# Experts in teams of four with 32 places each, instead of teams of two with 64

## The chip, the cores and the metric

The kernel runs on one core of a Trainium2 chip. The metric is the device time in microseconds. A core has TensorE (PE, the matmuls; PEld is its weight load), VectorE (DVE), ScalarE (ACT), GpSimd (POOL) and SyncE (SP, which here issues every DMA), with a scratch memory of 128 partitions (SBUF) and eight accumulation banks of 128 x 512 f32 (PSUM, `ps` in the code). The engines run their own instruction streams and wait for each other with semaphores.

## The reference, cut to what matters

Two transformer blocks over 256 tokens of 1024 channels. The change touches the mixture of experts of the second block: each token picks one of four groups, and in it two of eight experts, so 512 pairs of token and expert fall on 32 experts.

```python
def hierarchical_moe(h, rg_w, rg_b, re_w, re_b, w_gate, w_up, w_down):
    xt = h.reshape(S, D)                                  # 256 x 1024
    g_logits = xt @ rg_w + rg_b                           # 4 groups
    g_top = argmax(g_logits);  g_w = softmax(g_logits)[g_top]
    e_in = (xt @ re_w + re_b).reshape(S, 4, 8)[g_top]
    e_val, e_loc = top_k(e_in, 2)
    e_w = softmax(e_val) * g_w
    e_idx = g_top * 8 + e_loc
    for every expert e, for its tokens t:                 # 32 experts
        hb = silu(xt[t] @ w_gate[e]) * (xt[t] @ w_up[e])  # 1024 -> 256
        y[t] += (hb @ w_down[e]) * weight                 # 256 -> 1024
h = h + y
h = h + sigmoid(rms_norm(h) @ ple_gate_w) * (p @ ple_proj_w)
return rms_norm(h)
```

Each expert has 3 MB of f32 weights, 96 MB in all; every one is read, whatever the routing.

## The kernel before, in words

Before the experts stand the first block and the mixers of the second. Their matmuls are split by hand: weights and data are each taken as a high and a low part (fp32r), and three products are summed (`mm3`, L1268). That part is the same in both kernels.

**Routing.** PE computes the router's logits; DVE (`routing`, L1850) makes one-hot tables, counts each token's rank in its expert, and from it a place. `FEW` (64) places belong to each expert and `TEAM` (2) experts to a team, so that a team has 128 places, one for each row of the PE array's output. The largest count of each team goes to `route_i`; each engine reads it (`busiest`, L349) and, if it is over `FEW`, runs a loop for the rest (`extra`, L1680, L1103, L2271). `psel` is the matrix that picks the tokens of two teams (256 places), made by DVE (`select`); `places` and `weighed` (`placed`, L2304, with `weigh`, L1940) take the results back to the tokens.

**Loading.** SP loads each team's weights in `CHUNKS` (3) chunks of 2048 KB: two for gate and up (`w_eg`), one for down (`w_ed`), each 8 KB to a partition and expert. `wring` has six slots, the chunks of two teams. A slot is loaded again when PE has raised `chunk_used` for it (L510). The first six chunks are loaded while the block before still runs. After the experts' chunks SP issues two loads of `w_ple`.

**The loop over 16 teams** (L1725 on PE, L1127 on ACT, L2318 on DVE). PE in order: `gate_up` for two chunks, 16 matmuls of 512 columns in f32, one for each expert and 128 channels, with the tokens as the stationary operand. Expert j writes rows 64 j to 64 j + 63 of bank 4, so each matmul uses 64 columns of the array. Then `gather(b + 2)` picks half of the channels for a pair of teams, 16 matmuls of 256 columns into banks 5 and 6. Then it transposes `he`, which ACT (silu, L1130) and DVE (the product, L2321) have made. Then comes `combine` of the team before (16 matmuls into banks 0 to 3, where the sum over all experts stands), and last `down`, 8 matmuls of 512 columns into banks 6 and 7. ACT copies banks 6 and 7 to `yh` and DVE makes the low part `yl`. A plain f32 matmul stands in the trace as two records, an fp32r one as one.

**After the loop**: the last `combine`; ACT loads its table (L1138) and splits `w_ple` (high part, L710), DVE makes the low part (L720), adds the experts' sum to `hs` (L2339), and the last matmuls and two norms follow.

Of the kernel before, what the change touches and what calls it, by code (L numbers as in the profile page):

```python
# [41 lines left out]
FEW = 64  # L42
# [5 lines left out]
CHUNKS = 3  # L48
GU_CHUNKS = 2
# [70 lines left out]
for _name, _n in CONST:  # L120
# [17 lines left out]
        "dve": ["firsts", "select", "seconds", "comb", "moved", "xb", "he", "y"]}  # L138


def bass_two_blocks(nc, a, out):
# [4 lines left out]
    with ctx:  # L146
# [11 lines left out]
        with ExitStack() as turn:  # L158
            wring = sb("wring", [P, 2 * CHUNKS, CHUNK], F32, turn)
# [54 lines left out]
        with ExitStack() as turn:  # L214
# [3 lines left out]
            psel = [sb(f"psel{i}", [P, NB, 2 * P], F32R, turn) for i in range(2)]  # L218
            pselx = sb("pselx", [P, NB, P], F32R, turn)
            moe_room = 2 * D + 2 * SEQ + 4 * NB * P + NB * P  # L220
# [67 lines left out]
        zero = take(SEQ)  # L288
        mixed = mix[:, :, :].rearrange("p a b -> p (a b)")
# [117 lines left out]
        class Over:  # L407


            def __init__(self, eng, turn, b):  # L410
                self.eng, self.turn, self.before = eng, turn, b * (ROUNDS - 1)
# [5 lines left out]
            def step(self, what):  # L417

                def after(ins):
                    ins.then_inc(sem("over_dve"), 1)  # L420
                    self.wait("dve", what)
                return after

# [4 lines left out]
        def _(sp_):  # L428
# [77 lines left out]
            def experts(b, c):  # L506

                slot = b % 2 * CHUNKS + c
                if b >= 2:
                    sp_.wait_ge(sem("chunk_used"), (b - 2) * CHUNKS + c + 1)  # L510
                team = slice(b * TEAM, (b + 1) * TEAM)
                src = a["w_eg"][team, :, c * 2048:(c + 1) * 2048] if c < GU_CHUNKS else a["w_ed"][team, :, :]
                sp_.dma_start(wring[:, slot, :].rearrange("p (e n) -> p e n", e=TEAM), src.rearrange("e p n -> p e n"))\
                   .then_inc(sem(f"chunk{slot}"), 16)
# [3 lines left out]
            for slot, i in ((0, 1), (1, 2), (2, 2), (3, 3)):  # L518
                done, count = tile_done("w_out", i)
                sp_.wait_ge(sem(done), count)  # L520
                experts(slot // CHUNKS, slot % CHUNKS)
            sp_.wait_ge(sem("wout_psum"), KD)
            for slot in (4, 5):
                experts(1, slot - CHUNKS)
            for b in range(2, TEAMS):
                for c in range(CHUNKS):
                    experts(b, c)
            for i, count in ((0, (TEAMS - 2) * CHUNKS + 1), (1, (TEAMS - 1) * CHUNKS)):
# [10 lines left out]
        def pool_groups(eng, chain, groups, done):  # L539

            for g in groups:
                eng.wait_ge(sem("h_ready"), 2 * g + 2)
                eng.wait_ge(sem("hp_padded"), 1)
# [50 lines left out]
        def conv(eng, chain, j, done):  # L594

            eng.wait_ge(sem("z_evac"), z_done("conv", j))
            eng.wait_ge(sem("zpre_padded"), 2)
# [10 lines left out]
        def _(pool):  # L608
            chain = Chain(pool, "pool_chain")
            pool.memset(ones[:, :], 1.0).then_inc(sem("ones_ready"), 1)  # L610
            pool.memset(nones[:, :], -1.0).then_inc(sem("ones_ready"), 1)
            pool.memset(hp[:, :, 0:PADT], 0.0).then_inc(sem("hp_padded"), 1)
            pool.memset(brow[0:NH, :], NEG).then_inc(sem("brow_ready"), 1)
            whole = mix[:, 0:2, :].rearrange("p a b -> p (a b)").bitcast(I32)
            pool.iota(whole[:, 0:2 * P], pattern=[[ROUNDS * P, 2], [1, P]], base=0, channel_multiplier=0)
# [6 lines left out]
            pool.tensor_copy(iota[:, :], whole[:, 0:2 * P]).then_inc(sem("iota_ready"), 1)  # L622
            pool.tensor_copy(ranks[:, :], whole[:, 2 * P:2 * P + NE + ROUNDS]).then_inc(sem("iota_ready"), 1)
# [5 lines left out]
                .then_inc(sem("sgw_masked"), 1)  # L629
# [19 lines left out]
            for s in range(2):  # L649
                pool.memset(zpre[s][0:ML_D, :, 0:3], 0.0).then_inc(sem("zpre_padded"), 1)  # L650
# [195 lines left out]
        def _(act):  # L846
# [12 lines left out]
            act.wait_ge(sem("iota_ready"), 2)  # L859
# [237 lines left out]
            def gathered(n):  # L1097
                act.wait_ge(sem("gathered"), 2 * n + 1)
                first = n % 2 * 4
                act.activation(xb[n // 2 % 2][:, first:first + 2, :].rearrange("p a n -> p (a n)"), ps[:, 5, :], ACT.Copy)\  # L1100
                   .then_inc(sem("xb_ready"), 1)

            def extra(b):  # L1103
                count = busiest(act, b)
                with act.If(count > FEW):
                    with act.Fori(0, ROUNDS - 1) as r:
# [10 lines left out]
                with act.Else():  # L1117
                    act.sem_inc(sem("over_act"), len(OVER["act"]) * (ROUNDS - 1))
# [1390 lines left out]
```

## Time and profile before

| | us |
|---|---|
| median of 3 timed runs | 1072.61 (1070.78 to 1072.77) |
| the profiled execution | 1068.52 |
| its span, first to last instruction | 1066.8 |
| PE busy in it | 974.7 (91%) |
| DVE, ACT, POOL busy | 540.2, 416.1, 155.6 |
| mean DMA rate, and in the experts' stage | 199 GB/s, 417 to 420 |
| first gate and up matmul, last down's end | 771.3, 1011.0 |

All positions in microseconds are from the start of the span. The page shows the span in 40 equal slices of 26.7 us; a digit is the busy share in tenths, and PEclk the share of TensorE's full clock that was granted. Busy time of PE is not PE at its peak. In the chain of waits, followed back from the last instruction, "issue" is time in which the engine waited for nothing that the profile shows.

### The profile page before, as it was taken

How to read it: one execution, taken by the hardware profiler on the slowest of the kernel's cores; microseconds unless marked ns; L12 is line 12 of the kernel's file. 1: busy time of each engine (PE TensorE's matmuls, PEld its weight loads, DVE VectorE, ACT ScalarE, POOL GpSimd, SP SyncE). 2: the span in 40 equal slices, each digit the busy share in tenths (PEclk: the TensorE clock that was granted, in tenths of full speed). 3: DMA queues.
4: the chain of work that ended last, by engine and by line, in shares of the span. 5: the costliest groups of instructions: out<-in, count | busy, mean ns of one | idle time of the engine just before them, and what ended most of it. 6: DMA issues, size and time to landing. Idle time of an engine off the chain costs nothing.

```text
span 1066.8 us, 16807 instructions
## 1 busy us (share of the span) xinstructions
PE 974.7 (91%) x6776; PEld 819.1 (77%) x6777; DVE 540.2 (51%) x986; ACT 416.1 (39%) x697; POOL 155.6 (15%) x216
## 2 busy tenths in 40 slices
PE   3799999998989999999969999879699999999876
PEld 2599999998869899999959999578454555545365
DVE  5655454438783655554463548574523333433254
ACT  4543333347575534434454556633211111111153
POOL 5432323011001433331120000000100000000000
PEclk8899999999989999999998999788899999999988
DMA  7435453568522254534543412049079999999601
GB/s 290 157 106 202 167 172 134 189 185 205 141 80 89 93 213 158 188 131 163 214 164 127 159 52 82 1 168 396 3 283 417 420 420 420 419 420 419 260 1 40
DMA packets 36797, 211.99 MB, mean 199 GB/s; under 512 B 2528, under 2 KB 16112, under 8 KB 17520
## 3 DMA queue, kind: packets, MB, share of 16 engines
q1 hardware_dynamic: 36720, 210.91, 52.4%
q8 instruction: 55, 0.90, 0.3%
q14 instruction: 22, 0.18, 0.1%
HBM read 209.83 MB, written 1.07 MB: 198 GB/s over the span
## 4 chain that ended last, share of the span: by engine, by line
PE 85%; DVE 7%; ACT 3%; issue 2%; POOL 2%; DMA 0%; POOLq 0%; DVEq 0%; ACTq 0%
PE ps L1268 49%; PE ps L1651 11%; PE ps L1665 5%; PE ps L1259 3%; PE ps L1674 3%; PE ps L1623 2%; PE ps L1199 2%; DVE wl L720 2%; PE ps L1624 1%; DVE mix L1779 1%; PE ps L1306 1%; PE ps L1372 1%; PE ps L1207 1%; PE ps L1609 1%; PE ps L1592 1%
## 5 line engine op out<-in xcount | busy, mean ns | idle before, releaser
L720 DVE TENSOR_TENSOR wl<-ring,wh 128x2048 fp32r<-128x2048 f32 (+3 forms) x106 | 210.3, 1987 | 193.9 <-ACT wh L710 193.9
L710 ACT ACTIVATE wh<-ring 128x2048 fp32r<-128x2048 f32 (+3 forms) x106 | 176.1, 1665 | 267.2 <-PE ps L1268 265.2
L1268 PE MATMUL ps<-xh,wh 128*128 128x256 f32 (+3 forms) x632 | 180.5, 286 | 6.4 <-DVE xl L2343 6.4
L1268 PE MATMUL ps<-xh,wl 128*128 128x256 f32 (+3 forms) x632 | 179.0, 283 | 0.0
L1268 PE MATMUL ps<-xl,wh 128*128 128x256 f32 (+3 forms) x632 | 178.8, 283 | 0.0
L1268 PEld LDWEIGHTS ps<-xh,wh 128*128 128x128 f32 (+3 forms) x632 | 117.6, 186 | 7.8 <-issue 7.5
L1268 PEld LDWEIGHTS ps<-xh,wl 128*128 128x128 f32 (+3 forms) x632 | 117.6, 186 | 0.1
L1268 PEld LDWEIGHTS ps<-xl,wh 128*128 128x128 f32 (+3 forms) x632 | 117.5, 186 | 0.0
L1268 PE MATMUL ps<-acth,wh 128*128 128x272 f32 (+1 forms) x352 | 101.1, 287 | 0.0
L1268 PE MATMUL ps<-actl,wh 128*128 128x272 f32 (+1 forms) x352 | 100.0, 284 | 0.0
L1268 PE MATMUL ps<-acth,wl 128*128 128x272 f32 (+1 forms) x352 | 100.0, 284 | 0.0
L1268 PE MATMUL ps<-xhT,wl 128*128 128x272 f32 x320 | 92.6, 289 | 0.0
L1268 PE MATMUL ps<-xlT,wh 128*128 128x272 f32 x320 | 92.2, 288 | 0.0
L1268 PE MATMUL ps<-xhT,wh 128*128 128x272 f32 x320 | 91.3, 285 | 0.0
L575 POOL TENSOR_TENSOR sq<-sq 128x256 f32<-128x256 f32 (+1 forms) x15 | 19.1, 1274 | 436.0 <-ACT sq L685 436.0
L2327 DVE TENSOR_TENSOR yl<-ps,yh 128x512 fp32r<-128x512 f32 x32 | 20.6, 686 | 91.3 <-ACT yh L1137 91.3
L1268 PEld LDWEIGHTS ps<-acth,wh 128*128 128x128 f32 x352 | 66.5, 189 | 0.2
L1268 PEld LDWEIGHTS ps<-acth,wl 128*128 128x128 f32 x352 | 66.1, 188 | 0.2
L1268 PEld LDWEIGHTS ps<-actl,wh 128*128 128x128 f32 x352 | 66.2, 188 | 0.0
L1651 PE MATMUL ps<-wring,xb_even 128*64 128x512 f32 x256 | 60.0, 607 | 4.1 <-issue 4.0
L1268 PEld LDWEIGHTS ps<-xhT,wh 128*128 128x128 f32 x320 | 60.4, 189 | 0.0
L1268 PEld LDWEIGHTS ps<-xlT,wh 128*128 128x128 f32 x320 | 60.1, 188 | 0.0
(402 smaller groups left out, 1859.5 us busy)
## 6 DMA issues: line engine op xcount, KB each, us to landing
wring<-in_w_eg SPq DMA_DIRECT2D x32, 2048.0 KB, 14.3
ring<-in_w_gu SPq DMA_DIRECT2D x22, 2048.0 KB, 8.2
wring<-in_w_ed SPq DMA_DIRECT2D x16, 2048.0 KB, 12.9
ring<-in_w_dn SPq DMA_DIRECT2D x16, 1408.0 KB, 6.1
ring<-in_w_z SPq DMA_DIRECT2D x7, 2048.0 KB, 7.7
ring<-in_w_out SPq DMA_DIRECT2D x4, 1152.0 KB, 5.2
ring<-in_w_q SPq DMA_DIRECT2D x8, 512.0 KB, 6.2
ring<-in_w_o SPq DMA_DIRECT2D x8, 512.0 KB, 16.0
```

Of the source, the lines that this page charges most:

```text
L575: pool.tensor_tensor(even, even, odd, ALU.add).then_inc(sem("sq_paired"), 1)
L710: ins = act.activation(to, src, ACT.Copy)
L720: ins = dve.tensor_tensor(to, src, h.bitcast(F32), ALU.subtract)
L1199: pe.matmul(ps[:, 2 * j + g, 0:n], w[:, k * 256 + g * P:k * 256 + g * P + P], xa[:, k, 0:n], start=(k == 0 and part == 0), stop=False)
L1207: ins = pe.matmul(ps[:, 2 * j + g, 0:n], w[:, k * 256 + g * P:k * 256 + g * P + P], xb[:, k, 0:n], start=False, stop=(k == KD - 1))
L1259: mm(ps[:, 6, 0:n], ones[0:rows, :], square_at(name, c + 1 - chunks)[0:rows, 0:n], start=(c < chunks), stop=(c == last))\
L1268: ins = mm(o, p, q, start=first and n == 0, stop=last and n == 2)
L1623: mm(out, h2h[:, k, at], select[:, k, :], start=(k == 0), stop=False)
L1651: ins = mm(ps[rows, 4, :], x[:, k, rows], chunk(b, c)[:, j, i * 512:(i + 1) * 512], start=(k == 0), stop=(k == KD - 1))
L1665: ins = mm(ps[rows, 6 + i, :], heT[:, k, rows], chunk(b, GU_CHUNKS)[:, j, k * D + i * 512:k * D + (i + 1) * 512], start=(k == 0), stop=(k ...
L1674: ins = mm(ps[:, c // 2, c % 2 * SEQ:(c % 2 + 1) * SEQ], y[:, c * P:(c + 1) * P], weights, start=False, stop=last and y is parts[-1], skip ...
L2327: dve.tensor_tensor(yl[:, i * 512:(i + 1) * 512], ps[:, 6 + i, :], yh[:, i * 512:(i + 1) * 512].bitcast(F32), ALU.subtract).then_inc(sem(" ...
```

## The change

A team is now four experts with 32 places each. The chunks of a team are six (four for gate and up, two for down), each of 4 KB to a partition and expert, and `wring`'s six slots are one team. The matmuls of the experts use 32 columns of the array each. `psel` is single; a team's 256 places are two sets of 128, the first 32 tokens of each of its experts and the next 32, and both are gathered always (`PARTS`, four pieces, one behind each chunk of gate and up). If a team's largest count is over 32, each engine runs the team's body with a second pass on the second set (`twice`); the loop for the rest runs over 64, as before. `combine` of the team before stands behind the first chunk of gate and up. The code has both bodies, one for each way of the branch. The rest of the diff renames and merges semaphores and shifts the tables of places.

```diff
-FEW = 64
+FEW = 32
 TEAM = P // FEW
 TEAMS = NE // TEAM
 ROUNDS = SEQ // FEW
-CHUNKS = 3
-GU_CHUNKS = 2
+CHUNKS = 6
+GU_CHUNKS = 4
+PARTS = 4
...
-            wring = sb("wring", [P, 2 * CHUNKS, CHUNK], F32, turn)
+            wring = sb("wring", [P, CHUNKS, CHUNK], F32, turn)
...
             def experts(b, c):
-                slot = b % 2 * CHUNKS + c
-                if b >= 2:
-                    sp_.wait_ge(sem("chunk_used"), (b - 2) * CHUNKS + c + 1)
+                if b:
+                    sp_.wait_ge(sem("chunk_used"), (b - 1) * CHUNKS + c + 1)
                 team = slice(b * TEAM, (b + 1) * TEAM)
-                src = a["w_eg"][team, :, c * 2048:(c + 1) * 2048] if c < GU_CHUNKS else a["w_ed"][team, :, :]
+                name, at = ("w_eg", c * D) if c < GU_CHUNKS else ("w_ed", (c - GU_CHUNKS) * D)
...
-            for i, count in ((0, (TEAMS - 2) * CHUNKS + 1), (1, (TEAMS - 1) * CHUNKS)):
+            for i, count in ((0, (TEAMS - 1) * CHUNKS + 1), (1, (TEAMS - 1) * CHUNKS + 3)):
...
+            def team(b, twice):                            # PE
+                x = xb[b % 2]
+                for c in range(GU_CHUNKS):
+                    chunk_ready(b, c)
+                    if c == 0:
+                        pe.wait_ge(sem("xb_ready"), 2 * b + 2)
+                        pe.wait_ge(sem("xb_ready_d"), 2 * b + 2)
+                    if twice:
+                        ins = gate_up(c, x[:, :, P:2 * P], 6)
+                        if c == GU_CHUNKS - 1:
+                            ins.then_inc(sem("second_pe"), 1)
+                    gate_up(c, x[:, :, 0:P], 4).then_inc(sem("chunk_used"), 1)
+                    if c == 0 and b:
+                        pe.wait_ge(sem("y_ready"), 2 * b)
+                        pe.wait_ge(sem("y_low"), 2 * b)
+                        pe.wait_ge(sem("places_ready"), b)
+                        combine((yh, yl), places[(b - 1) % 2][:, :])
+                    if b + 1 < TEAMS:
+                        if c == 0:
+                            pe.wait_ge(sem("psel_ready"), b + 2)
+                        gather(b + 1, c)
+                pe.wait_ge(sem("he_ready"), b + 1)
+                transposes(he, 4).then_inc(sem("het_psum"), 1)
+                if twice:
+                    second(pe, "dve", "he", b)
+                    transposes(he2, 6).then_inc(sem("second_pe"), 1)
+                pe.wait_ge(sem("heT_ready"), b + 1)
+                if twice:
+                    second(pe, "act", "heT", b)
...
+                for k in range(2):
+                    chunk_ready(b, GU_CHUNKS + k)
+                    if twice:
+                        ins = down(k, heT2, (4, 6))
+                        if k == 1:
+                            ins.then_inc(sem("second_pe"), 1)
+                    down(k, heT, (5, 7)).then_inc(sem("chunk_used"), 1)
+                if twice:
+                    second(pe, "act", "y", b)
+                    second(pe, "dve", "y", b)
+                    combine((yx,), combx).then_inc(sem("second_pe"), 1)
...
             for b in range(TEAMS):
+                count = busiest(pe, b)
+                extra(b, count)
+                with pe.If(count > FEW):
+                    team(b, True)
+                with pe.Else():
+                    pe.sem_inc(sem("second_pe"), len(SECOND["pe"]))
+                    team(b, False)
...
+            def team(b, twice):                            # ACT
+                if b + 1 < TEAMS:
+                    gathered(b + 1)
+                act.wait_ge(sem("chunk_used"), b * CHUNKS + GU_CHUNKS)
+                act.activation(sgate, ps[:, 4, 0:FE], ACT.Silu).then_inc(sem("sg_ready"), 1)
...
+                if twice:
+                    second(act, "pe", "down", b)
+                    act.activation(yx[:, 0:512], ps[:, 4, :], ACT.Copy).then_inc(sem("second_act"), 1)
...
+            def team(b, twice):                            # DVE
+                if b + 1 < TEAMS:
+                    gathered(b + 1)
+                if twice:
+                    dve.wait_ge(sem("chunk_used"), b * CHUNKS + 1)
+                    step("slot")(dve.tensor_scalar(small[:, 182:183], small[:, 176:177], float(P - P * ROUNDS), None, ALU.add))
+                    weigh(dve, step("parts"), combx, 182, 183).then_inc(sem("second_dve"), 1)
+                dve.wait_ge(sem("sg_ready"), b + 1)
+                dve.scalar_tensor_tensor(he, ps[:, 4, FE:2 * FE], small[:, 178:179], sgate, ALU.mult, ALU.mult)\
+                   .then_inc(sem("he_ready"), 1)
...
+                for i in range(2):
+                    dve.wait_ge(sem("y_ready"), 2 * b + i + 1)
+                    dve.tensor_tensor(yl[:, i * 512:(i + 1) * 512], ps[:, 5 + 2 * i, :], yh[:, i * 512:(i + 1) * 512].bitcast(F32),
+                                      ALU.subtract).then_inc(sem("y_low"), 1)
+                if twice:
+                    second(dve, "pe", "down", b)
+                    dve.tensor_copy(yx[:, 512:D], ps[:, 6, :]).then_inc(sem("second_dve"), 1)
+                if b + 1 < TEAMS:
+                    dve.wait_ge(sem("he_ready"), b + 1)
+                    placed(b + 1)
+                if b + 2 < TEAMS:
+                    selected(b + 2)
```

How instructions stand now. PE of before, the end of gate and up of the first team and its gather, transposes and down (one row is one f32 or fp32r matmul; `x7` are seven alike; in brackets the semaphores that it waits for):

```order
L1651 MATMUL ps<-wring,xb_even 64x512 [waits chunk1]
L1651 MATMUL ps<-wring,xb_even 64x512 x7
L1623 MATMUL ps<-psel,h2h 128x256 [waits xb_ready_d,xb_ready,psel_ready]
L1624 MATMUL ps<-psel,h2l 128x256
...
L1657 MATMUL ps<-cst,work 128x128 [waits he_ready]
L1657 MATMUL ps<-cst,work 128x128
L1665 MATMUL ps<-wring,work 64x512 [waits chunk2,xb_ready_d,heT_ready]
L1665 MATMUL ps<-wring,work 64x512 x7
```

The whole gather of 16 stands in one piece between gate and up and the transposes there. PE of after, the same place of the first team, in the body of two passes:

```order
L1677 MATMUL ps<-wring,xb_even 32x512 [waits chunk3]
L1677 MATMUL ps<-wring,xb_even 32x512 x15
L1648 MATMUL ps<-psel,h2h 128x256 [waits xb_ready_d]
L1649 MATMUL ps<-psel,h2l 128x256
...
L1683 MATMUL ps<-cst,work 128x128 [waits he_ready]
L1683 MATMUL ps<-cst,work 128x128
L1683 MATMUL ps<-cst,work 128x128 [waits second_dve]
L1683 MATMUL ps<-cst,work 128x128
L1690 MATMUL ps<-wring,work 32x512 [waits xb_ready_d,xb_ready,chunk4,second_act,heT_ready]
L1690 MATMUL ps<-wring,work 32x512 x15
L1690 MATMUL ps<-wring,work 32x512 [waits chunk5]
L1690 MATMUL ps<-wring,work 32x512 x15
L1698 MATMUL ps<-work,mix 128x256 [waits second_dve,second_act]
L1698 MATMUL ps<-work,mix 128x256 x7
```

A chunk has 16 matmuls in two passes (8 in one), a quarter of the gather follows it, and the combination of the second pass (L1698, plain f32) stands behind the last down. On DVE, the same body of after for the third team:

```order
L2316 COPY xb_even<-ps 128x512 [waits gathered] x2
L2376 TENSOR_SCALAR small<-small 128x1 [waits chunk_used]
L1991 SCALAR_TENSOR_TENSOR work<-work,small 128x256 [waits second_dve]
L1992 SCALAR_TENSOR_TENSOR work<-work,small 128x256
L1993 SCALAR_TENSOR_TENSOR work,small<-work 128x256 [waits second_dve]
L2379 SCALAR_TENSOR_TENSOR work<-ps,small,work 128x256 [waits sg_ready]
L2385 TENSOR_TENSOR work<-work,ps 128x256 [waits second_act]
L2388 TENSOR_TENSOR yl<-ps,yh 128x512 [waits y_ready] x2
L2392 COPY mix<-ps 128x512 [waits second_pe]
```

The weighing of the second pass (L1991 to L1993) stands between the copy of the last gathered part and `he` (L2379); before, the copy stood behind `he`.

## Rows read from the trace of the kernel before

**Rows 1.** The page's forty slices: the DMA engines' busy share in tenths.

```profile
DMA  7435453568522254534543412049079999999601
```

**Rows 2.** Stretches: length, busy us of each engine, granted clock, DMA share, GB/s.

```profile
740.00:760.00 20.00, 15.75 (x71) 13.52 (x72) 11.22 (x49) 6.92 (x15) 2.35 (x4) 0.76 0.34 140
860.00:880.00 20.00, 20.00 (x110) 9.41 (x108) 7.84 (x22) 3.54 (x7) 0.00 (x0) 1.00 1.01 419
980.00:1000.00 20.00, 17.71 (x90) 7.59 (x88) 6.86 (x21) 2.94 (x6) 0.00 (x0) 1.00 0.99 406
```

**Rows 3.** SP's DMA issues in order of time; landing times of all chunks.

```profile
779.45 3.80 SPq L513 DMA_DIRECT2D wring<-in_w_eg  x2
863.18 0.37 SPq L513 DMA_DIRECT2D wring<-in_w_ed  x1
877.87 0.37 SPq L513 DMA_DIRECT2D wring<-in_w_ed  x1
DMA to landing us min/median/max: 7.9/13.9/18.8
```

**Rows 4.** The chain of waits: start, us, what; records.

```profile
767.38 1.73 PE ps L1721 x4
...
863.14 6.87 PE ps L1651 x32
870.00 0.32 PE ps L1623
...
872.12 0.22 PE ps L1657 x2
872.33 1.91 PE ps L1674 x16
874.25 3.58 PE ps L1665 x16
```

**Rows 5.** The chain at the first team.

```profile
772.37 1.75 issue
774.12 8.72 PE ps L1651 x30
```

**Rows 6.** DVE in order of time behind a down that ended at 863.13.

```profile
865.02 0.47 DVE L1943 SCALAR_TENSOR_TENSOR work<-work,small 128x256 f32<-128x256 f32 x1
866.39 0.29 DVE L2309 TENSOR_SCALAR places<-work 128x256 fp32r<-128x256 f32 x1
867.76 0.88 DVE L1936 SCALAR_TENSOR_TENSOR psel<-iota,small,psel 128x256 fp32r<-128x256 f32 x2
870.53 0.48 DVE L2321 SCALAR_TENSOR_TENSOR work<-ps,small,work 128x256 f32<-128x256 f32 x1 [0.42 <-ACT work L1130]
872.15 0.69 DVE L2268 COPY xb_even<-ps 128x512 f32<-128x512 f32 x1 [1.13 <-PE ps L1624]
```

**Rows 7.** The chain's end of the stage, and PE's last combination there.

```profile
1007.40 3.61 PE ps L1665 x16
1012.13 1.28 ACT L1138
1013.43 1.92 ACT wh L710
1015.37 4.49 DVE wl L720 x2
1013.05 0.38 PE L1674 MATMUL ps<-places,yh 128*128 128x256 f32 x1 [2.07 <-ACT yh L1137]
1016.22 0.41 PE L1674 MATMUL ps<-places,yl 128*128 128x256 f32 x1
```

**Rows 8.** Weight loads of experts (ns min/median/max) and combinations (group, mean ns).

```profile
L1651 PEld LDWEIGHTS ps<-wring,xb_even x256: 132/137/231, 771.3 to 972.8; 128*64 128x64 f32 x128
L1674 PEld LDWEIGHTS ps<-places,yl 128*128 128x128 f32 x120 | 23.0, 191 | 0.0
```

**Rows 9.** DMA issues of w_o: count, KB each, median us to landing.

```profile
ring<-in_w_o SPq DMA_DIRECT2D x8, 512.0 KB, 16.0
```

More of the change, by code:

```diff
@@ L138 @@
         "dve": ["firsts", "select", "seconds", "comb", "moved", "xb", "he", "y"]}
+SECOND = {"pe": ["gu", "het", "down", "done"], "act": ["sg", "heT", "y"], "dve": ["slot", "parts", "comb", "he", "y"]}
 def bass_two_blocks(nc, a, out):
@@ L288, in bass_two_blocks @@
         zero = take(SEQ)
+        sgate2 = take(FE)
+        he2 = wproj[:, 2048:2048 + FE]
+        heT2 = take(FE // P, P)
         mixed = mix[:, :, :].rearrange("p a b -> p (a b)")
@@ L1095, in _, with gathered, extra @@
             act.preload_act_table_set("silu_and_others")
[L1097 to L1106, printed above, removed]
+            def gathered(b):
+                for part in range(0, PARTS, 2):
+                    act.wait_ge(sem("gathered"), PARTS * b + part + 1)
+                    act.activation(xb[b % 2][:, 2 * part:2 * part + 2, :].rearrange("p a n -> p (a n)"), ps[:, 5, :], ACT.Copy)\
+                       .then_inc(sem("xb_ready"), 1)
+            def extra(b, count):
+                with act.If(count > 2 * FEW):
+                    with act.Fori(0, ROUNDS - 2) as r:
                         over = Over(act, r, b)
@@ L1625, in pick, with gather @@
                 return ins
-            def gather(n):
-                for half in range(2):
-                    for i in range(2):
-                        ins = pick(ps[:, 5 + half, i * 2 * P:(i + 1) * 2 * P], n % 2 * 4 + half * 2 + i, psel[n // 2 % 2])
-                    ins.then_inc(sem("gathered"), 1)
+            def gather(b, part):
+                if part >= 2:
+                    pe.wait_ge(sem("xb_ready_d" if part % 2 else "xb_ready"), 2 * b + part // 2)
+                for i in range(2):
+                    ins = pick(ps[:, 5 + part % 2 * 2, i * 2 * P:(i + 1) * 2 * P], 2 * part + i, psel)
+                ins.then_inc(sem("gathered"), 1)
             def gather_extra():
@@ L1678, in combine, with extra @@
                 return ins
[L1680 to L1682 removed]
+            def extra(b, count):
+                with pe.If(count > 2 * FEW):
                     for c in range(CHUNKS):
@@ L2263, in _, with gathered, extra @@
             routing(dve, chain)
[L2265 to L2274 removed]
+            def gathered(b):
+                for part in range(1, PARTS, 2):
+                    dve.wait_ge(sem("gathered"), PARTS * b + part + 1)
+                    dve.tensor_copy(xb[b % 2][:, 2 * part:2 * part + 2, :].rearrange("p a n -> p (a n)"), ps[:, 7, :])\
+                       .then_inc(sem("xb_ready_d"), 1)
+            def extra(b, count):
+                with dve.If(count > 2 * FEW):
+                    if b:
+                        second(dve, "pe", "done", b - 1)
+                    with dve.Fori(0, ROUNDS - 2) as r:
                         over = Over(dve, r, b)
```

231 lines of the change are left out of this document (103 added, 128 removed).

## The prediction

> **What bounds the kernel now.** I read the page's forty slices first, and look for where DMA is full. From slice 30 to 37 the sixteen DMA engines stand at 9 [rows 1]. These are the experts: 48 chunks of 2048 KB, of which the first six are loaded earlier. Then the stretches: 860 to 880 us has PE busy for all 20 us and 419 GB/s moved [rows 2]. Both are full, so I need the period of each. SP issues the down chunk of one team at 863.18 and of the next at 877.87, so a team of two experts takes 14.7 us [rows 3]. A chunk is 2.097 MB, which at 420 GB/s is 4.99 us; three are 15.0 us. PE's own work for a team is, in the chain, 6.87 for gate and up, about 1.9 for the gather, 0.4 for the transposes, 1.91 for the combination and 3.58 for down: 14.7 [rows 4]. So PE sets the pace, 0.3 us a team ahead of what DMA can hold: the refills land 7.9 us after their issue at first and up to 18.8 us at the end [rows 3]. If PE's work fell to nothing, DMA alone would still need 42 x 4.99 = 210 us from its first refill, issued at 779.45. The end of this stage in the profiled execution is the last down, 1007.40 + 3.61 = 1011.0 [rows 7]; what follows it (table load, split of w_ple, the adds) starts from there. The profiled execution took 1068.52 us, 1.7 more than its span and 4.1 less than the median of the three timed runs, 1072.61. I make the sum on the profiled one and carry the difference over.
>
> **How many teams go twice.** This is not in the profile; it follows from the inputs. Counting the reference's own routing, the largest expert of each team of four has 57, 30, 19, 21, 19, 8, 40 and 40 tokens. Teams 0, 6 and 7 are over 32 and take the second pass; none is over 64, so neither the loop of before nor that of after runs. That the last two teams are both twice is what decides.
>
> **Price of a matmul.** An f32 matmul of 512 columns over the whole array is 1.73 / 2 = 0.865 us. With 64-wide tiles the chain has 16 of them (32 records, two each) in 6.87 us: 0.43 each, so two run side by side at no loss [rows 4]. No row has four side by side. The far ends are 0.215 each (all four overlap) and 0.43 each (only two do). I take 0.215, from the nearest row: the pair loses nothing, and the array's columns are as separate in quarters as in halves. What could stand between is weight loading: a load takes 137 ns at 64 columns and 191 at 128, so at 32 columns some 110 by the slope; four in a row would be 0.44 us against 0.43 for a pass, that is nothing, and 4 x 0.137 = 0.55 if it stayed at the 64-wide price [rows 8]. That last price, 1.10 us for a group of four instead of 0.86, is the second rival below.
>
> The Trainium skill (TensorE: Matmul & The Clock Gate, "Measured speedup vs the span model") has a table with a gain of 3.07 times for four row tiles and 2.38 for three column tiles. By it, as an estimate, a group of four would take 4 x 0.865 / 3.07 = 1.13 us and the sum would come out near that rival's. No run here shows it for four; for pairs this trace shows no loss, 0.43 us a matmul.
>
> **PE's work after, per team of four.** A chunk is 8 matmuls: 8 x 0.215 = 1.72 us. Six chunks 10.3; the gather is unchanged per expert, 32 matmuls at 0.12 = 3.9 (16 lie from 870.00 to 872.12 in the chain [rows 4]); the combination once a team instead of twice, 1.9; transposes 0.3. Sum 16.4 us, against 2 x 14.7 = 29.4 before and 6 x 4.99 = 29.9 for DMA. With a second pass come 10.3 again, 0.3, and the combination of yx, 8 plain f32 matmuls of 256 columns, 8 x 0.43 = 3.5: 30.4 us. So a team taken once leaves PE waiting for DMA nearly half of the time, and a team taken twice is heavier than DMA before any wait is counted. Waits of a twice team, in PE's order: the transposes wait for he, which DVE reaches after the copy of the last gathered part (0.69), the slot and the weighing (865.02 to 866.39 = 1.4, plus 0.3 for the slot), then he (0.5): 3.3 us with the hand-overs [rows 6]. heT and heT2 cost 0.9. The combination of yx waits for ACT's third copy and DVE's copy behind its two subtractions: 2.8. Sum 37.4 us. Team 7 has no gather, so the weighing is done early (he costs 1.1), and the combination lies behind its last down: 23.1 + 1.1 + 0.9 = 25.1 to the end of down.
>
> **Teams 0 to 5.** The first refill: chunk 0 takes 16 half-width matmuls now and 16 quarter-width then (both passes), 3.5 us warm either way, behind the same gap of 1.75 us and the same slow start (30 records in 8.72 us where 6.5 would do [rows 5]). So its issue stays at 779.4 and its landing at 787.3. Further chunks of team 0 are used every 3.4 + 1.0 = 4.4 us, in time; but the fifth comes after the 3.3 and 0.9 of waits, at 801.5, and lands at 809.4 where 807.3 was due, 2.1 late; team 1 starts at 805.0 + 2.8 + 3.5, its first chunk lands 1.5 late. Teams 1 and 2 work off the backlog, with 1.9 us each for psel: DVE makes it 5.5 us behind down (yl, weighing, places, select [rows 6]), PE asks for it after 3.6. From team 3 on PE waits for landings and DMA never stops. Chunk 37, the first of team 6, lands at 787.3 + 30 x 4.99 + 3.6 = 940.6. The last down then ends at 940.6 + 37.4 + 25.1 = 1003.1, 7.9 us sooner than before.
>
> **What is lost again.** The clock: before the last combination PE stood idle for 2.07 us, and the 16 matmuls from 1013.05 to 1016.6 went at 0.21 each, not 0.12: 1.2 GHz instead of 2.4, 16 x 0.09 = 1.4, with what came before it some 1.7 us lost for one such pause [rows 7]. The kernel of after has these pauses in each twice team: at he (3.3) and at yx (2.8) in team 6, at he (1.1, then 0.9) in team 7: 3 x 1.7 = 5.1. The pauses of team 0 cost 3.4, of which I pass 2.0 on to DMA. Branches: each team now has two conditionals, and bodies for both ways; the gap of 1.75 us at the first team is of this kind and is not covered [rows 5]. Elsewhere the running ahead of PE's queue covers it if PE has work left, which in a backlog is 1.7 us of down: I take 1.5 in all, between 0 and 3 x 1.75.
>
> The Trainium skill (TensorE: Matmul & The Clock Gate, "HAM oscillation") says that bursts of matmuls with waits for DMA between them fall back to the slow clock each time. By that rule teams 3 to 5 would run slow at times too; as an estimate that costs nothing, since DMA covers most of it, and the sum stays. The trace agrees as far as it goes: after work with gaps the stretch 740 to 760 has the clock at 0.76 [rows 2].
>
> The end: ACT has a third copy (0.6) before its table load at 1012.13, so the split of w_ple and all behind it start 0.6 later; the combination of yx and the last one (3.5 + 1.9, at half clock up to 10) still end before DVE has split (1.28 + 1.92 + 4.49 in a row [rows 7]). w_ple's first half lands one chunk behind the last expert's, before ACT wants it.
>
> Sum: 1003.1 + 5.1 + 2.0 + 1.5 = 1011.7, against 1011.0; with 0.6 at the end +1.3 us. Profiled 1069.8; median 1073.9. The large saving on PE goes where DMA sets the pace, and the last two teams spend what is left.
>
> **DMA's pieces.** A chunk had 256 rows of 8 KB, now 512 of 4 KB. w_o is the only transfer in 4 KB rows, to 64 partitions: 512 KB took 16.0 us to land, queued behind others; an expert's chunk took 13.9 in the median for four times as much, also queued [rows 3, 9]. Those are far ends: nothing, or a DMA of twice the time (+150 us). I take nothing; 4 KB into 128 partitions is nearer to the experts' chunk. Each 1% would be 1.5 us.
>
> **Rivals.** (a) The pauses stay too short to cost the clock, and branches are hidden: 1003.1 + 0.6 = 7.3 less than 1011.0, which is 1065.3 on the median's scale, as all times here. For it: between 980 and 1000 PE was idle for 20 - 17.71 = 2.3 us in all, in shorter pauses, and the clock stayed at 1.00 [rows 2]; against it: the 2.07 us. 0.22. (b) Four tiles' weight loads queue up: 1.10 us for each of the 24 groups of matmuls in a twice team, 0.24 more each = 5.8; teams 6 and 7 in full, team 0 through its late refills: 3 x 5.8 = 17, so 1091. It ends slower, and decides alone from a group's time over about 0.9 us. For it: the loads are not seen to get shorter than 0.132; against it: those of a pair start together and cost nothing. 0.10. (c) Only pairs overlap: 0.43 a matmul, so a twice team costs 2 x 10.3 = 20.6 more; three of them 62, and the others at 26.7 and their waits fall behind DMA by some 13 in all: +75, 1148. Nothing in the rows speaks for it except that no more than two were ever seen. 0.07. (d) DMA loses by 4 KB rows, +6 or more. 0.02. The forecast has 0.59.
>
> **Numbers.** The forecast's own terms (clock 2 to 10, branches 0 to 5, team 0) give it 1067 to 1082. 8 in 10, with most of (a) and (b) taken in: 1065 to 1091. What a measurement can tell from no change is 0.2%, 2.1 us. Of the forecast's 0.59 I put 0.09 under -2.1, 0.24 within, 0.26 over. Faster 0.22 + 0.09 = 0.31; same 0.24; slower 0.26 + 0.10 + 0.07 + 0.02 = 0.45.
>
> **What will show it.** Groups of four f32 matmuls every 0.86 us on PE; SP's waits in teams 3 to 5 for use right behind landing; DMA at 419 or more up to about 995 with two dents near 805 and 815; PE busy near half in teams 2 to 5 and a clock under 1.00 in places; idle 3.3 us before he2's transposes in teams 0 and 6; the last down ending between 1003 and 1018. I am wrong if the last down ends before 1001 (team 6 and 7 cheaper than 62 us), or if the groups take over 1 us.

## The result, and the profile after

The changed kernel takes 1096.95 us (median of 4 runs, 1093.78 to 1097.89) where the kernel before took 1071.69 in the same comparison: a ratio of 1.0241, 95% interval 1.0211 to 1.0272. It is slower by 2.4%. The prediction was 1073.9, within 1065 to 1091, and the time lies outside that range. The profiled execution has a span of 1095.1 us.

The page's slices of the DMA engines, as in [rows 1]:

```profile
DMA  7335454478324255345624311183568999999401
```

Where before went from 0 in slice 29 to 7 and then 9, this climbs over 5, 6 and 8 (slices 29 to 31) and DMA is full only from slice 32; slice 38 is emptier, too. The span is longer, so a slice is 27.4 us here. The stretches of [rows 2] (length, busy us of PE, PEld, DVE, ACT, POOL, granted clock, DMA share, GB/s), and two of the gaps that the chain shows:

```profile
860.00:880.00 20.00, 8.75 (x70) 3.21 (x72) 6.32 (x20) 2.45 (x5) 0.00 (x0) 0.79 1.03 405
811.80:820.10 8.30, 0.03 (x5) 0.05 (x5) 0.55 (x4) 0.00 (x0) 0.00 (x0) 0.81 0.31 115
965.50:1005.84 40.34, 34.47 (x264) 15.69 (x252) 12.76 (x39) 5.23 (x11) 0.00 (x0) 0.96 1.03 408
1010.50:1038.30 27.80, 26.12 (x212) 9.22 (x212) 2.28 (x7) 1.39 (x5) 0.00 (x0) 0.92 0.51 193
```

In the middle PE is busy for 8.75 of 20 us and DMA is full at 405 GB/s, not 419. Half of PE's time was forecast to be free there, but for waits for landings; here 9.6 of the 11 idle us are the one gap at 869.11 in the chain below. From 811.8 to 820.1 neither works. Team 6 takes 40.3 us and team 7 27.8.

The chain of waits from the end of the first team to the last down (start, us, what; compare [rows 4] and [rows 5]):

```profile
808.12 3.69 PE ps L1698 x16
811.81 8.27 issue
820.08 3.64 PE ps L1677 x16
...
826.79 1.85 PE ps L1677 x16
...
841.52 6.33 issue
847.85 3.47 PE ps L1677 x16
...
869.11 9.60 issue
878.71 3.40 PE ps L1677 x16
...
931.78 10.21 issue
941.99 3.64 PE ps L1677 x16
...
960.24 5.31 PE ps L1690 x32
965.55 3.97 PE ps L1677 x32
...
1002.15 3.69 PE ps L1698 x16
1005.84 4.72 issue
1010.56 5.75 PE ps L1677 x32
...
1031.15 7.11 PE ps L1690 x64
```

Two things are to be seen. Eight matmuls of a quarter of the array (16 records) take 1.85 us, 0.23 each, and 32 of them (64 records) 7.11, 0.22 each: the four do run side by side. And at each boundary between teams but one PE stands in "issue", that is, it waits for nothing that the profile knows: for 4.7 to 10.2 us. (At the start of the fifth team it is 6.10 and then, in the middle of its first chunk, 2.68 more.) The exception is 965.55. In the table of waits (us in all, times, the longest) this is by far the largest row, and no wait for a landing stands in it:

```profile
PE ps L1677 <- issue: 50.3, 8, 10.2
```

What stands there on PE's sequencer are the branches. Its rows for L1682 of before (skip the extra loop), and for L1705 (the same) and L1795 (choose the team's body) of after (count: duration in ns, min/median/max):

```profile
L1682 PEldq COMPARE_BRANCH  x16: 220/319/3215, 770.8 to 993.4; - x16
```

```profile
L1705 PEldq COMPARE_BRANCH  x8: 343/2122/6876, 771.4 to 1003.2; - x8
L1795 PEldq COMPARE_BRANCH  x11: 70/379/7536, 772.1 to 1041.0; - x11
```

In time order, the one at L1705 takes 5.15 us at 809.37, and the one at L1795 takes 5.04 at 814.73, 7.54 at 840.01, 7.38 at 871.03, 7.31 at 898.39 and 7.30 at 934.39: the five teams of one pass, each behind a jump over the body of two. L1705 has three more long ones: 3.79 at 867.03, 4.47 at 929.70 and 6.88 at 1003.23, so the gap of 8.27 us is two jumps in a row, and the last gap, 4.72, is one over the extra loop. No branch of DVE or ACT took over 1 us in the stage. The gap-free boundary is the one where a team of one pass, whose body stands second, is followed by a team of two, whose body stands first: there the program runs straight on, jumping over nothing but the extra loop. I read this as PE waiting for its own code; in 4 us of one of these branches (842.5 to 846.5) the DMA queue of PE's instructions shows

```profile
q8 instruction: 2, 0.03, 5.8%
```

that is, two packets of 16 KB, taking 1.5 and 2.2 us beside the weights' packets. Single packets of this queue, of about 1.1 us, come all through the stage, in before too. Two at once stand nowhere in before's stage; in after they stand in each of the five long branches at L1795 and in the one of 6.88 us at L1705.

### The profile page after: what moved, and what is told of

Read it like the earlier page. It is cut to its first block, busy times and chain, and to the rows that moved or that the text cites. A ratio compares the mean times of both kernels' runs of the same rounds, so it can differ in the third digit from the quotient of the medians.

```text
span 1095.1 us, 16979 instructions
## 1 busy us (share of the span) xinstructions
PE 941.7 (86%) x6974; PEld 790.5 (72%) x6975; DVE 514.5 (47%) x908; ACT 404.6 (37%) x674; POOL 156.4 (14%) x216
## 4 chain that ended last, share of the span: by engine, by line
PE 80%; DVE 8%; issue 6%; ACT 4%; POOL 2%; DMA 0%; POOLq 0%; DVEq 0%; ACTq 0%
PE ps L1293 48%; PE ps L1677 8%; PE ps L1690 4%; PE ps L1284 3%; PE ps L1698 2%; PE ps L1648 2%; PE ps L1224 2%; DVE wl L728 1%; PE ps L1649 1%; DVE mix L1827 1%; PE ps L1331 1%; PE ps L1397 1%; PE ps L1232 1%; PE ps L1634 1%; PE ps L1617 1%
## 5 line engine op out<-in xcount | busy, mean ns | idle before, releaser
L1677 PE MATMUL ps<-wring,work 128*32 128x512 f32 x320 | 44.2, 691 | 32.8 <-issue 32.8
L1677 PE MATMUL ps<-wring,xb_even 128*32 128x512 f32 x384 | 50.1, 644 | 17.5 <-issue 17.5
L1293 PEld LDWEIGHTS ps<-xhT,wl 128*128 128x128 f32 x320 | 60.2, 188 | 0.0
```

What stands on the lines that cost most here:

```text
L1293: ins = mm(o, p, q, start=first and n == 0, stop=last and n == 2)
L1677: ins = mm(ps[rows, bank, :], x[:, k, rows], chunk(c)[:, j, i * 512:(i + 1) * 512], start=(k == 0), stop=(k == KD - 1))
```

## The experiments

All times are medians with the ratio to the kernel before on the same chip and its 95% interval. An f32 matmul is four instructions on PE (two weight loads, two matmuls), an fp32r matmul two, so the body of two passes is some 540 instructions, the one of one pass some 300, the extra loop's body some 300 in after and some 200 in before.

**e1_static.** The branch between two bodies goes, on PE as shown and on ACT and DVE alike:

```diff
-                with pe.If(count > FEW):
-                    team(b, True)
-                with pe.Else():
-                    pe.sem_inc(sem("second_pe"), len(SECOND["pe"]))
-                    team(b, False)
+                if b not in TWICE:                         # TWICE = (0, 6, 7)
+                    pe.sem_inc(sem("second_pe"), len(SECOND["pe"]))
+                team(b, b in TWICE)
```

> The kernel after, with the teams that take the second pass (0, 6, 7) written into the program instead of a branch on the count; the rest as in after. Theory (jumps): on PE each team of after jumps over a body that is not taken, and that jump stood for 4.7 to 10 us in its trace, 8.3 of it ahead of team 1 with DMA idle and about 11 ahead of team 6. Without them team 6 starts some 11 us earlier and team 7 4.7 earlier again: the last down ends near 1019 instead of 1038, the time is 1078 (1073 to 1083). Rival (size of the second passes and the 4 KB rows, jumps hidden by DMA as in the prediction): at most 4 us less than after, 1093 or more.

Measured: 1078.4, 1.0107 (1.0074 to 1.0141), against 1.0241 of after. The last down ended at 1017.2 in its trace (expected 1019), the first chunk of team 6 landed at 950.0 (962.6 in after). So the branches between the bodies cost 14 us of the 26 by the two ratios, 18.5 by the two medians. The extra loop's jump still takes 4.7 and 6.0 us in two places, and the gaps at the teams' starts are down from 50.3 us to

```profile
PE ps L1675 <- issue: 13.0, 4, 5.3
```

**e2_never_twice.** `TWICE = ()`, the rest as e1.

> As e1_static, and no team takes the second pass (leaves out the tokens beyond the 32nd of an expert). Both theories: DMA alone sets the stage. 42 chunks at 5.09 us from a first refill near 776, with some 5 us of late landings, so the last chunk lands near 998 and the last down ends near 1001: 1059 to 1062. If the quarter-array matmuls or the single gather of once-teams were themselves too slow, PE would not wait for landings and the time would stay over 1066. The difference to e1_static is the price of the three second passes at their places: 17 to 19 us by the jump theory; by the rival e1 stays at 1093 and the difference is over 30.

Measured: 1061.9, 0.9940 (0.9916 to 0.9963). The last chunk landed at 998.9 and the last down ended at 1002.6. With one pass PE waits for landings in nearly every team: DMA alone sets the stage. The three second passes cost 1.7% where they stand. (This kernel leaves out the tokens beyond an expert's 32nd; it prices the passes and computes something else.)

**e3_short_ifs.** Choice by the count as in after, but with one body:

```diff
-                    if twice:
+                    with pe.If(count > FEW):
                         ins = gate_up(c, x[:, :, P:2 * P], 6)
...
-                with pe.If(count > FEW):
-                    team(b, True)
-                with pe.Else():
-                    pe.sem_inc(sem("second_pe"), len(SECOND["pe"]))
-                    team(b, False)
+                team(b, count)
```

> The kernel after with the same choice by the count, but on PE one body for a team, in which only the matmuls of the second pass stand in branches of their own (eight short ones), instead of two whole bodies. Theory (a jump costs when its target is far, because the code there has to be fetched: two fetches of 16 KB stand in each of after's stalls): the stalls at the teams' ends go, some of the extra loop's (4 to 6 us, one to three times) stay, eight short branches cost 0.4 us each beside PE's work. So within 4 us of e1_static, 1076 to 1083. Rival (each branch costs some us wherever it leads, eight of them eight times): slower than after, over 1100.

Measured: 1084.6, 1.0173 (1.0138 to 1.0208): 0.7% faster than after, 0.7% slower than e1, a little above what was expected. The short branches themselves are cheap. The extra loop's are not (first line: L1705, to skip the extra loop; second: L1745, over the second pass of a chunk):

```profile
L1705 PEldq COMPARE_BRANCH  x8: 326/2731/6178, 772.4 to 994.1; - x8
L1745 PEldq COMPARE_BRANCH  x32: 65/208/1162, 773.2 to 1006.6; - x32
```

Five of the eight jumps over the extra loop's 300 instructions now take 2.1 to 6.2 us, where two did in e1. The loop's body is the same; what differs is where it lies.

**e4_order.** e1 with another order of teams:

```diff
+ORDER = (1, 0, 2, 6, 3, 7, 4, 5)
...
-                team = slice(b * TEAM, (b + 1) * TEAM)
+                team = slice(ORDER[b] * TEAM, (ORDER[b] + 1) * TEAM)
...
-            return eng.value_load(route_i[0:1, b:b + 1], min_val=0, max_val=SEQ)
+            return eng.value_load(route_i[0:1, ORDER[b]:ORDER[b] + 1], min_val=0, max_val=SEQ)
```

> As e1_static, with the teams in the order 1, 0, 2, 6, 3, 7, 4, 5 (loads, table of places, counts), so that the three with a second pass stand between teams without one. Theory: a second pass in the middle is hidden by DMA (a twice-team is 10 us over DMA's 30.5, a once-team behind it 10 under), so the time is near that of e2_never_twice: 1060 to 1064. Rival: the second passes cost the same wherever they stand, because the slots are returned late: as e1_static, 1078.

Measured: 1070.1, 1.0011 (0.9991 to 1.0032). That is 1% faster than e1, but not the 1060 to 1064 expected. I had let a once-team win back what a twice-team loses; it does not win back enough. PE starts the stage six chunks behind: by the third team in order it used its first chunk 20 us after it landed, so slots came back too late: the landings of chunks 28 to 31 are 6.7, 6.2, 8.0 and 7.0 us apart and those of 42 and 43 9.1 and 6.8, instead of 5.11. Two jumps over the extra loop stand there as well, 6.25 us at 858.15 and 6.17 at 968.66, the second right ahead of the issue of chunk 42; what each cause costs was not tried apart. This trace is of the second slowest of ten executions (1075.3).

**e6_before_4k.** Before, with the DMAs of after:

```diff
-                team = slice(b * TEAM, (b + 1) * TEAM)
-                src = a["w_eg"][team, :, c * 2048:(c + 1) * 2048] if c < GU_CHUNKS else a["w_ed"][team, :, :]
+                four = slice(b // 2 * 4, b // 2 * 4 + 4)
+                at = (b % 2 * GU_CHUNKS + c) * D if c < GU_CHUNKS else b % 2 * D
+                src = a["w_eg" if c < GU_CHUNKS else "w_ed"][four, :, at:at + D]
```

> The kernel before with the DMAs of after: each 2048 KB chunk is read as 4 KB rows of four experts instead of 8 KB rows of two (each weight is still read once, but the matmuls take the wrong ones). Theory: chunks land every 5.09 us instead of 4.96, the stage turns from PE-bound to DMA-bound, the last landing moves by 41 x 0.13 = 5 us: +3 to +5 us, 1075 to 1077. Rival (the slower landings of after came from its code loads or its stalls, not from the rows): no change, 1071.7 within 0.2%.

Measured: 1069.8, 1.0013 (0.9995 to 1.0030): no change in time where 3 to 5 us were expected, so the step from the rows to the time missed. The time is what the rival gave, but the rival's cause is refuted: the rate did fall with the rows alone; the stretch of [rows 2] in this kernel:

```profile
860.00:880.00 20.00, 20.00 (x110) 9.38 (x108) 9.85 (x31) 3.40 (x7) 0.00 (x0) 1.00 1.02 408
```

408 GB/s instead of 419, chunks 5.11 us apart instead of 4.96. PE is busy for all 20 us in both. The last chunk landed at 998.5 against 997.0, although this run's first refill was issued 3.1 us earlier; the trace is of the fastest of ten executions (1065.3). The row size costs DMA 3%, and before, with six slots loaded ahead, did not wait for it.

**e7_near_jump and e8_far_jump.** The jump by itself. Before, with a body that is never taken, of n = 1 (32 instructions) and of n = 18 (576):

```diff
                 with pe.Else():
                     pe.sem_inc(sem("over_pe"), len(OVER["pe"]) * (ROUNDS - 1))
+                with pe.If(count > SEQ - 8):
+                    for _ in range(n):
+                        gate_up(b, 0, xbx)
```

> The kernel before with a body of 8 matmuls that is never taken (condition: over 248 tokens) on PE at the start of each of the 16 teams: one more short jump a team. Theory (distance decides): a branch of 0.4 us ahead of work already queued, no change to +5 us: 1070 to 1076. Rival (every taken jump refetches): +50 us or more.

> As e7_near_jump with 144 matmuls in the dead body, about the size of the body of after with two passes. Theory: every team pays a stall of 4 to 7.5 us and PE sets the pace here, so 16 x 5 to 16 x 7 = +80 to +110 us less what the queue ahead of PE covers (1 to 2 us each): 1120 to 1175. Rival (after's stalls come from DMA or semaphores at the teams' ends): as e7_near_jump.

Measured, with two executions each: near 1081.5, 1.0130 (1.0098 to 1.0162); far 1174.3, 1.0999 (1.0957 to 1.1041). The new branch's rows on PE's sequencer, first near, then far:

```profile
L1707 PEldq COMPARE_BRANCH  x16: 213/213/3651, 771.2 to 1009.4; - x16
```

```profile
L1707 PEldq COMPARE_BRANCH  x16: 4374/6828/7749, 773.1 to 1097.7; - x16
```

A jump over 576 instructions is dear each of the 16 times: 6.8 us in the median, 4.4 at the least. Two 16 KB packets at once stand in each of the 16, as in after's. The chain of far shows what of it reaches PE:

```profile
793.97 5.60 issue
799.57 9.01 PE ps L1651 x32
...
812.81 3.58 PE ps L1665 x16
816.40 4.57 issue
820.97 8.55 PE ps L1651 x32
```

4.6 to 5.6 us of pause, and the gate and up behind it takes 8.6 to 9.0 us where 6.87 stood before [rows 4], at a granted clock of 0.83 and 0.78. That is 6.3 to 7.7 us a team. From the second team to the last the new branches lie 21.9 us apart where before had 14.8: 15 x 7.1 = 106, and 107 were measured. Near missed its expectation (0 to 5 us; 14 measured). Its own branch takes 0.21 us in the median and 2.9 and 3.7 at two teams; the old one over the extra loop (200 instructions, not touched) took 6.0, 5.9 and 3.6 us at three teams where before had one of 3.2. So adding code changes which of the short jumps are dear; that they are those that leave the code at hand is my reading, not shown.

**e9_combined, e13_repaired.** e3's short branches, with two pauses of the second pass taken out:

```diff
+                if twice:                                   # DVE, now ahead of gathered(b + 1)
+                    dve.wait_ge(sem("chunk_used"), b * CHUNKS + 1)
+                    ...
+                    weigh(dve, step("parts"), combx, 182, 183).then_inc(sem("second_dve"), 1)
                 if b + 1 < TEAMS:
                     gathered(b + 1)
...
+                with pe.If(count > FEW):
+                    for k in range(2):
+                        chunk_ready(b, GU_CHUNKS + k)
+                        ins = down(k, heT2, (4, 6))
+                    ins.then_inc(sem("second_pe"), 1)
                 for k in range(2):
                     chunk_ready(b, GU_CHUNKS + k)
-                    if twice:
-                        ins = down(k, heT2, (4, 6))
-                        if k == 1:
-                            ins.then_inc(sem("second_pe"), 1)
                     down(k, heT, (5, 7)).then_inc(sem("chunk_used"), 1)
```

ACT and DVE copy `yx` ahead of `yh` and `yl`. e9 has e4's order too, e13 the order of after.

> e3_short_ifs with the team order of e4_order, and in a team with a second pass: DVE makes the weighing before it copies the last gathered part, and PE does the second pass of both down chunks ahead of the first pass, so that yx is copied while PE works. It still chooses by the count and is right for any routing. Theory: a second pass costs some 2 us less at he and 3 to 4 less at yx, the chunks come free sooner, and DMA's pauses at the second and third of them (landings of 6.2 to 9.1 us apart instead of 5.11, 12 us in all in e4_order) mostly go: 1061 to 1066, that is 0.3 to 0.8% faster than before. Rival (these pauses come from the far jumps of the extra loop, 6.2 us twice in e4_order): no more than 3 us gained on e4_order, 1067 or more.

> e9_combined in the teams' own order, so teams 6 and 7, both with a second pass, stand last again: the change with short branches, the weighing ahead of the gathered copy and the second pass of down first. Theory: against e3_short_ifs (1.0173 of before) it saves the pauses of each second pass, 5 to 6 us a time (2 at he, 2.7 and a slow clock at yx). In teams 6 and 7 nothing hides that, in team 0 half: 10 to 13 us, so 1072 to 1076, 1.003 to 1.008 of before. The distance to e9_combined (0.998), 6 to 10 us, is then what two heavy teams at the end cost. Rival (the order is what gained in e9_combined, not the pauses): within 4 us of e3_short_ifs.

Measured: e9 1065.8, 0.9979 (0.9962 to 0.9996), just faster than before, by 0.2% where 0.3 to 0.8 was expected; e13 1073.9, 1.0054 (1.0032 to 1.0076), still slower, as expected. In e9's table of waits PE no longer waits for the copy of `yx` (8.2 us over three teams in after) and for `he` 9.2 us instead of 12.2; the largest row left is

```profile
PE ps L1680 <- issue: 24.3, 8, 4.8
```

**e10_no_branches.** e9 with positions 1, 3 and 5 written in as the teams of two passes, and the extra loop left out.

> As e9_combined with the teams of two passes written into the program (positions 1, 3 and 5) and the extra loop for over 64 tokens left out on every engine (no team needs it here): no branch stands between the teams. Theory (what is left of e9_combined's loss is the far jumps of the extra loop: five of 3.9 to 6.6 us, 26 us of PE's sequencer): the last chunk lands near 1000 instead of 1004.5, as in e2_never_twice, 1059 to 1063. Rival (these jumps are hidden by DMA, as they are where it is behind): within 2 us of e9_combined, 1064 to 1067.

Measured: 1057.5, 0.9880 (0.9849 to 0.9911). No branch stands between the teams, PE waits for landings again, 38 of the 41 steps from the first refill's landing are 5.07 to 5.14 us, and the last chunk is there at 997.8. It beats both kernels, for this routing alone. Against e9 the branches cost 1%: five dear ones over the extra loop (26.2 us of the sequencer) and the short ones, which this run does not tell apart.

**e11_rows_8k, e12_both.** Chunks of two experts in 8 KB rows on top of e9 and of e10; PE takes them two at a time:

```diff
-                name, at = ("w_eg", c * D) if c < GU_CHUNKS else ("w_ed", (c - GU_CHUNKS) * D)
+                first = ORDER[b] * TEAM + c % 2 * 2
+                name, at = ("w_eg", c // 2 * 2 * D) if c < GU_CHUNKS else ("w_ed", 0)
...
-                              a[name][team, :, at:at + D].rearrange("e p n -> p e n")).then_inc(sem(f"chunk{c}"), 16)
+                              a[name][first:first + 2, :, at:at + 2 * D].rearrange("e p n -> p e n")).then_inc(sem(f"chunk{c}"), 16)
```

> As e9_combined with chunks of two experts in 8 KB rows instead of four in 4 KB rows; PE takes two chunks at a time (16 matmuls of a pass), so slots come free in pairs. Theory: a chunk lands every 4.96 us instead of 5.11 wherever DMA never waits, up to 6 us in all; PE's coarser steps give 2 to 4 back (16 instead of 8 matmuls behind the last landing, two chunks needed at a team's start): 1062 to 1066. Rival (the coarse steps weigh more: slots wait for each other): 1068 or more.

> e10_no_branches with the chunks of e11_rows_8k. If both theories hold, the gains add, since both make DMA's stream shorter and PE has slack: 1056 to 1060, 1% faster than before. If DMA's stream in e10 is already held up by PE, it is the same as e10 or slower.

Measured: e11 1069.1, 1.0005 (0.9975 to 1.0035); e12 1056.6, 0.9878 (0.9849 to 0.9907). e11 missed: no gain, a loss if anything. It is no clean test of the rows, since its trace has a dear short branch that e9's lacks (5.8 us at 836.03). e12's time is in its expected range, but it cannot be told from e10. Its stream is shorter by what was expected: with the first refill landing at 785.2 in both, the last lands at 991.9 instead of 997.8. But the last down ends only 2.8 us earlier (997.0 against 999.8), with twice the matmuls behind the last landing. 8 KB rows are worth 6 us of DMA time here; the coarse steps that this form needs take back half of it by the last down, and the times do not show the rest.

## Why the prediction was wrong, point by point

- **What bounds the kernel before**: right. Before kept its time with a DMA 3% slower (e6). (The page's full slices are 31 to 37; slice 30 has a 7.)
- **Which teams go twice**: right; the long teams are 0, 6 and 7.
- **Price of a matmul**: 0.215 us predicted, 0.22 to 0.23 measured (7.11 for 32, 1.85 for 8), so a group of four is 0.89 to 0.93. The rivals with 1.10 and more fell. The table in the Trainium skill that I weighed there (TensorE: Matmul & The Clock Gate, "Measured speedup vs the span model") would have given an estimate of 1.13 for this group; the trace has 0.89 to 0.93.
- **Team 6, team 7**: 37.4 and 25.1 us without the clock, 62.5 in all, with 3.4 and 1.7 for the clock 67.6. Measured 40.3 and 27.8, 68.1. Right in kind, waits at he and yx included (3.3 and 2.8 forecast, 2.6 and 2.7 measured); that the sum fits to 0.5 us is partly luck. The clock's part came in other places: the combination of `yx` at 1002.15 ran at full speed (3.69), but team 6's down, behind the wait at he, took 8.80 instead of 7.11, and gate and up of team 7, behind the jump, 5.75 instead of 3.57.
- **DMA's pieces**: taken at nothing, measured 5.11 instead of 4.96 a chunk. Of the 41 refills that is 6 us, of the 30 up to team 6 4.5. It was a rival with 0.02; it happened, with the 6 us of DMA time named there, though in the kernel before they cost nothing (e6).
- **Branches**: this step failed. The prediction took 1.5 us in all, "between 0 and 3 x 1.75", from the one gap that the chain showed, at the first team [rows 5]. That gap was no branch's: it lies between two matmuls of gate and up, from 772.37, and before's branch there took 0.22 us at 770.79. Measured were branches of 3.8 to 7.5 us at nine places, 54.9 us of PE's sequencer. e1 takes the new one away (L1795, 34.6 of them) and gains 14 to 18 us; e8 makes such a jump by itself, 6.8 us each. The mistake was to price a branch without what it jumps over. The new one leads over 300 or 540 instructions, and the diff showed it: two whole bodies, one of them always jumped over.
- **Where it reached the end**: up to the start of team 6. Forecast was 940.6 + 2.0 + 1.5 = 944.1, measured 965.5, 21.4 later. The landings say where (chunks 6 to 36). At the first boundary DMA had run dry at 816.1, and the next issue waited for the gap of 8.27 us: the landing came 17.3 us after the one before it, at 833.3. Over the six steps up to there 16.2 us were lost to 5.11 a step, where the sum had 5.6: 10.6 more, 8.3 of it the two jumps. Slower rows give 30 x (5.11 - 4.99) = 3.6. Three late landings (7.6, 7.8 and 6.6 us behind the one before, chunks 15, 25 and 35, the first chunk being 0) give 6.7. Team 6 itself started 2.9 us after its first landing, since team 5 had been held up by its 10.2 us gap, where 1.5 stood for branches. With the first landing 0.8 earlier that is 10.6 + 3.6 + 6.7 + 1.4 - 0.8 = 21.5. Behind team 6 came the gap of 4.72. The other gaps (6.3, 9.6, 8.8 and 10.2 at teams 2 to 5) cost little on their own: DMA had work queued, and but for the late ones above its landings stayed 5.1 us apart. But PE's spare time went into these gaps. The forecast had it wait for landings from team 3 on, and in after it never did.
- **The sign and the rivals**: slower had 0.45 and came, but the forecast was slower by 0.1% for other reasons, so the sign is luck. None of the rivals was this mechanism, and neither of the two signs of being wrong (a last down before 1001, groups over 1 us) would have shown it; the last down, at 1038.3, ended 20 us behind the window of 1003 to 1018. "Branches are hidden" stood inside the best case (a) and a few us in the forecast, and no case had them dear.

A rule of the Trainium skill bears on the step that failed, and I had not weighed it (Runtime: NRT & Kernel Launch, "Instruction fetch mechanics"): code is fetched ahead in sequence in 16 KB blocks, and a taken branch whose target is not in the two blocks at hand waits for a DMA. By that rule a jump over a body longer than two such blocks always stalls. The page also gives PE four times the instruction memory of most engines, and does not say whether PE's window is wider. The traces agree with the narrow one: jumps over 540 and 576 instructions stalled 21 times of 21, with two instruction packets of 16 KB in each. They give the price that the page does not: 6.8 us in the median of e8.

What the traces of before did show, and I did not use: its branch over the extra loop took 0.2 to 0.4 us fifteen times and 3.2 us once, at 993.37. A single long one among short ones was the sign that the price is not in the branch.

**What stays open.** Why three landings in after are 1.5 to 2.7 us late was not tried apart; before has two of that kind (6.35 and 6.30 against 4.96) and e2 two (6.54 and 6.38). And how the 300 or 200 instructions of the extra loop's body must lie to be cheap was not tested: it was 0.3 us in one place and 6 in another of the same program. That the pauses are the fetch of code rests on the packets that stand in them, and on their growth with the distance of the jump; nothing here changed the fetch by itself.

## What to carry to other kernels

Count the instructions that a branch jumps over, on each engine, before you price it: here 32 mostly cost 0.2 us, 200 to 300 between 0.3 and 6.9, and 576 6.8 in the median and 4.4 at the least, plus a slow clock behind it. Where two cases share most of their work, write one body with short branches around the difference (0.7% here), or take the case out of the program. And where PE and DMA are nearly balanced, look at where the heavy items stand: the same work was 1.0107 of before with two heavy teams last, 1.0011 with them spread, and 0.9880 when the pauses and jumps were gone as well.

## What the runs showed of the hardware that was not expected

- Four f32 matmuls on quarters of the array's columns run at once at 0.89 to 0.93 us for the group, against 0.87 for a single one over the whole array.
- Where DMA is full, a 2 MB load in rows of 4 KB lands every 5.10 to 5.12 us, in rows of 8 KB every 4.96 to 4.97 (408 and 419 GB/s), by the median steps of five traces of the one kind and four of the other.
- A jump over 576 instructions costs PE 6.6 to 7.7 us of sequencer time beside weight loads (fourteen of e8's sixteen), and 4.4 where DMA is idle (773.13). In after the one over 540 with DMA nearly idle, at 814.73, took 5.0, the other four 7.3 to 7.5.
- 32 instructions of dead code in each team cost 1.3% in all, more of it at an untouched branch, three times dear instead of once, than at their own.
